# Last attention head with its softmax one step deeper, and the first expert's products in plain float32

## The reference

```python
logits = jnp.einsum('thd,tnhd->thn', q, k_sel).astype(jnp.float32) * ATT_HEAD_DIM ** -0.5
p = jax.nn.softmax(logits + bias, axis=-1)
o_att = jnp.einsum('thn,tnhd->thd', p, v_sel)
x = x + mix @ w_out                       # mix: retention heads and attention heads side by side
# for the 128 rows that an expert takes at a time:
hid = jax.nn.silu(xb @ w_gate[e]) * (xb @ w_up[e])
out = hid @ w_down[e]
```

## Time and profile before

| | |
|---|---|
| median of three runs | 1246.58 us (1245.07 to 1246.71) |
| the profiled execution's own time | 1249.32 us |
| its span in the trace | 1247.5 us |
| PE busy | 1137.8 us, 91% |
| DVE, ACT, POOL busy | 855.7, 692.5, 233.2 us |
| mean granted clock of PE | 0.958 of full |

### The profile page before, as it was taken

How to read it: one execution, slowest core, us unless ns; L and a number is a source line. 1 busy time by engine, 2 the same in 40 slices (tenths; PEclk the granted TensorE clock), 3 DMA queues, 4 the chain that set the end, 5 groups by cost and what they waited for, 6 DMA issues and landing times.

```text
span 1247.5 us, 18108 instructions
## 1 busy us (share of the span) xinstructions
PE 1137.8 (91%) x6481; PEld 938.6 (75%) x6481; DVE 855.7 (69%) x1763; ACT 692.5 (56%) x1191; POOL 233.2 (19%) x275
## 2 busy tenths in 40 slices
PE   5997899999999999999999789997699999999955
PEld 5984477888777987888887468886578888888832
DVE  6439878788888767333343532446899999999935
ACT  6347577787878142443433431113378888888822
POOL 1320024343333100000000000000233333343112
PEclk8999899999999899999999899997799999999978
DMA  8252030404030242444224534003699999999756
GB/s 283 41 118 28 29 98 1 110 1 110 1 87 1 58 131 60 111 119 109 78 70 133 170 105 179 34 35 135 224 403 397 397 386 395 394 391 391 285 206 279
DMA packets 129536, 205.35 MB, mean 165 GB/s; under 512 B 17396, under 2 KB 102804, under 8 KB 117156
## 3 DMA queue, kind: packets, MB, share of 16 engines
q1 hardware_dynamic: 114852, 177.61, 41.0%
q0 software_dynamic: 12864, 21.02, 5.4%
q10 hardware_dynamic: 1728, 5.51, 1.1%
HBM read 182.02 MB, written 34.37 MB: 173 GB/s over the span
## 4 chain that ended last, share of the span: by engine, by line
PE 76%; DVE 11%; ACT 4%; DMA 4%; issue 3%; SPq 1%; POOL 0%; DVEq 0%; POOLq 0%; ACTq 0%
PE psum L2239 5%; PE psum L2241 5%; PE psum L2512 5%; PE psum L2514 4%; PE psum L2240 4%; PE psum L2513 4%; DVE place L1481 3%; PE psum L2387 3%; PE psum L2389 3%; PE psum L2211 3%; PE psum L2388 3%; PE psum L2212 2%; PE psum L2213 2%; PE psum L2531 2%; PE psum L2533 2%
## 5 line engine op out<-in xcount | busy, mean ns | idle before, releaser
L1902 DVE TENSOR_TENSOR place<-place,place 128x2048 fp32r<-128x2048 f32 x64 | 146.2, 2286 | 9.8 <-ACT place L1272 9.8
L1095 ACT ACTIVATE place<-place,place 128x768 uint8<-128x768 f32 (+3 forms) x128 | 125.5, 983 | 6.7 <-DVE place L1512 6.7
L2239 PE MATMUL psum<-place,place 128*128 128x512 f32 x288 | 121.9, 423 | 2.4 <-DVE place L1469 2.4
L1272 ACT CAST place<-place 128x2048 fp32r<-128x2048 f32 x64 | 122.3, 1915 | 0.0
L2241 PE MATMUL psum<-place,place 128*128 128x512 f32 x288 | 113.4, 394 | 0.0
L2240 PE MATMUL psum<-place,place 128*128 128x512 f32 x288 | 112.6, 391 | 0.0
L2512 PE MATMUL psum<-place,place 128*128 128x512 f32 x256 | 106.7, 417 | 0.0
L2514 PE MATMUL psum<-place,place 128*128 128x512 f32 x256 | 101.4, 396 | 0.0
L2513 PE MATMUL psum<-place,place 128*128 128x512 f32 x256 | 101.0, 394 | 0.0
L2211 PE MATMUL psum<-place,place 128*128 128x256 f32 x288 | 87.1, 303 | 3.5 <-ACT place L1117 3.5
L905 POOL TENSOR_TENSOR place<-place,place 128x1 f32<-128x1 f32 x9 | 5.1, 565 | 428.1 <-DVE place L1862 428.1
(11 more groups left out here) (329 smaller groups left out, 3107.3 us busy)
## 6 DMA issues: line engine op xcount, KB each, us to landing
place<-in_w_gate SPq DMA_DIRECT2D x32, 1024.0 KB, 7.6
place<-in_w_up SPq DMA_DIRECT2D x32, 1024.0 KB, 9.9
place<-in_w_down SPq DMA_DIRECT2D x32, 1024.0 KB, 10.7
place<-in_w_in SPq DMA_DIRECT2D x28, 512.0 KB, 6.4
place<-expert_out SPq DMA_DIRECT2D x9, 1024.0 KB, 13.9
place<-in_cache_attn_k SPq DMA_DIRECT2D x32, 256.0 KB, 3.1
place<-in_cache_attn_v SPq DMA_DIRECT2D x32, 256.0 KB, 3.4
place<-in_x_prompt SPq DMA_DIRECT2D x3, 1536.0 KB, 6.9
```

Of the source, the lines that this page charges most:

```text
L1095: last = nc.scalar.activation(reached[j], score[j], ACT.Sign, bias=pivot.bitcast(F32)[:, j:j + 1], scale=-1.0, accum_out=minus[:, j - BY_A ...
L1272: nc.scalar.copy(w_gu_hi[e % 2][:, :, ks, :], w_gu[e % 3][:, :, ks, :]).then_inc(w_hi_done, 1)
L1902: nc.vector.tensor_tensor(w_gu_lo[e % 3][:, :, ks, :], w_gu[e % 3][:, :, ks, :], w_gu_hi[e % 2][:, :, ks, :].bitcast(F32), ALU.subtract).t ...
L2239: nc.tensor.matmul(bank(4 + b), hT_hi[:, k, rows], hi, start=k == 0, stop=False)
```

## The change

**Last head.** With `lag(h)` = 1 for the last head alone, PE turns the probabilities two steps after the logits and multiplies by the values three steps after. DVE scales step i-1 (`scaled`) behind the maximum of step i. A third buffer `prob_third` is used in turn with the two, and the turned rows go to PSUM banks 4 and 5 in turn (`turned_bank`). ACT copies a block's first four turned tiles ahead of the exponents and the rest behind them. The loop is one step longer. `high_mix(0)` and `low_mix(0)` move from step 7 to step 5, ahead of the output weights; the chunks are spread over steps 5 to 10; and chunk 7 alone stands behind the last block's values on PE, where 6 and 7 stood. `w_out` comes in two loads of 2 MB: one ahead of the first four cached values, one ahead of the last four, and `g_ffn` behind them all.

**First expert.** Its rows are copied, not split (ACT half of them, DVE the other half, from the two PSUM banks), and so are its hidden rows. Its weights are not split. PE takes 8 plain float32 products for 24, and 4 for 12, with the next expert's rows turned between the fourth and the fifth. DVE computes the gates ahead of the split of expert 1's weights, and `rows_lo(1)` stands behind `over_slots`.

```diff
@@ last head: PE
+                late = lag(h)
+                for i in range(T + 2 + late):
...
-                    if h + 1 == AH and i in (8, 9):
-                        first_out(OUT_FILL[i])
-                    if 1 <= i <= T:
-                        turn_probs(i - 1, 0)
+                    x = i - late
+                    if 1 <= x <= T:
+                        turn_probs(x - 1, 0)
...
+                    if x >= 2 and x - 2 != SAMPLE:
+                        values(x - 2)
...
+                    if h + 1 == AH and i in OUT_FILL:
+                        filled = first_out(OUT_FILL[i])
@@ tables
-        OUT_SPLIT = {5: (0, 1), 6: (2, 3), 7: (4,), 8: (5,), 9: (6, 7)}
-        OUT_FILL = {8: (0, 1, 2), 9: (3, 4, 5), 10: (6, 7)}
+        OUT_SPLIT = {5: (0, 1), 6: (2,), 7: (3, 4), 8: (5,), 9: (6,), 10: (7,)}
+        OUT_FILL = {8: (0, 1, 2), 9: (3, 4), 10: (5, 6), 11: (7,)}
@@ last head: SP
-                    sp.dma_start(w_out, i_["w_out"][0].rearrange("(c p) n -> p c n", p=P)).then_inc(w_out_in, 16)
-                    sp.dma_start(g_ffn, ...).then_inc(w_out_in, 16)
                 for i in range(NB, 2 * NB):
+                    if h + 1 == AH and i in (NB, LATE_VALUES):
+                        x = int(i == LATE_VALUES)
+                        sp.dma_start(w_out[:, 4 * x:4 * x + 4], ...).then_inc(w_out_in[x], 16)
                     load_cached(h, i)
+                if h + 1 == AH:
+                    sp.dma_start(g_ffn, ...).then_inc(w_out_in[1], 16)
@@ last head: DVE
+                    if late and 1 <= i <= T:
+                        scaled(i - 1)
...
+                    if h + 1 == AH and i == 5:
+                        low_mix(0)
                     if h + 1 == AH and i in OUT_SPLIT:
...
-                    if h + 1 == AH and i == 7:
-                        low_mix(0)
@@ first expert: DVE
-            gate_up_lo(0, 0)
-            gate_up_lo(0, 1)
             L(v, gates_of(1, *PARTS[1]))
             gates_of(2, *PARTS[2]).then_inc(frames_done, 1)
             gate_up_lo(1, 0)
+            gate_up_lo(1, 1)
...
-            rows_lo(0)
-            gate_up_lo(1, 1)
-            rows_lo(1)
+            raw_rows()
...
             over_slots()
+            rows_lo(1)
@@ first expert: PE
+            def raw_gate_up():
+                pe.wait_ge(xT_hi_done, 1)
+                pe.wait_ge(gu_in[0], 32)
+                for k in range(KD):
+                    if k == KD // 2:
+                        gathered(1)
+                    last = nc.tensor.matmul(bank(0), xT_over[:, k, :], w_gu[0][:, :, k, :], start=k == 0, stop=k == KD - 1)
+                last.then_inc(gu_ps, 1)
```

More of the change, by code:

```diff
@@ L1181, in turned_probs @@
                     w = min(4, key_tiles(ORDER[i]) - 4 * m)
-                    nc.scalar.copy(probT[i % 2][:, 4 * m:4 * m + w, :], bank(5, 0, w * P)).then_inc(tp_read, 1)
-                for i in range(T + 2):
+                    nc.scalar.copy(probT[i % 2][:, 4 * m:4 * m + w, :], turned_bank(h, i, m)[:, 0:w * P]).then_inc(tp_read, 1)
+                late = lag(h)
+                for i in range(T + 2 + late):
                     if i < 4:
                         cached_columns(2 * i)
+                    if late and 2 <= i <= T + 1:
+                        turned_probs(i - 2, 0)
                     if i < T:
@@ L1198, in attention @@
                         cached_columns(2 * i + 1)
-                    if 1 <= i <= T:
+                    if not late and 1 <= i <= T:
                         for m in range(GROUPS[i - 1]):
                             turned_probs(i - 1, m)
+                    if late and 2 <= i <= T + 1 and GROUPS[i - 2] == 2:
+                        turned_probs(i - 2, 1)
                     if i < 4 and h + 1 == AH:
@@ L1696, in attention, with scaled @@
                 bias_mask(ORDER[0])
-                for i in range(T + 3):
+                late = lag(h)
+                def scaled(i):
+                    w = P * key_tiles(ORDER[i])
+                    v.wait_ge(ex_done, T * h + i + 1)
+                    nc.vector.reciprocal(inv_sum[i % 2], row_sum[i % 2]).then_inc(rs_done, 1)
+                    v.wait_ge(rs_done, T * h + i + 1)
+                    nc.vector.tensor_scalar(prob_of(h, i)[:, 0:w], prob_of(h, i)[:, 0:w], inv_sum[i % 2], None, ALU.mult).then_inc(pn_done, 1)
+                for i in range(T + 3 + late):
                     if i < T:
@@ L2502, in hidden, with raw_down @@
                 turn_hidden(hid[e % 2]).then_inc(hid_ps, 1)
+            def raw_gate_up():
[6 more added lines that the diff above has]
+                last.then_inc(gu_ps, 1)
+            def raw_down():
+                pe.wait_ge(hidT_done, 1)
+                pe.wait_ge(dn_in[0], 16)
+                for half_n in range(2):
+                    for k in range(2):
+                        last = nc.tensor.matmul(bank(6 + half_n), hidT_over[:, k, :], w_dn[0][:, k, 512 * half_n:512 * half_n + 512],
+                                                start=k == 0, stop=k == 1)
+                last.then_inc(dn_ps, 1)
             def gate_up(e):
@@ L2536, in _ @@
             gathered(0)
-            for e in range(NE):
+            raw_gate_up()
+            for e in range(1, NE):
                 if e + 1 < NE:
@@ L2542, in _ @@
                     over_frames()
-                if e >= 1:
+                    raw_down()
+                else:
                     down(e - 1)
```

104 lines of the change are left out of this document (58 added, 46 removed).

## The result

The changed kernel takes 1237.05 us (median of 10 runs, 1232.59 to 1242.54), the kernel before, run beside it, 1247.26 (10 runs, 1243.39 to 1248.66): a ratio of 0.9918, 95% interval 0.9905 to 0.9932, so 10.2 us less (8.5 to 11.8). The forecast was 1237.7. The profiled execution took 1236.26 us, its span is 1234.4 and PE's mean granted clock 0.969, for 1249.32, 1247.5 and 0.958 before.

A forecast was written before the change was run, and what follows sets the result against it. PE was taken to bound the long stages, so gains had to come from its waits and half clock. Last head 6.0 plus first experts 2.9 gave 8.9 us off the median 1246.58: 1237.7, range 1233.5 to 1243.5.

The forecast's parts named there:

- The queue on DVE: Last head: DVE does `low_mix(0)`, two chunks and the maximum of step 6 ahead of the scale of step 5.
- the place and length of the wait: Last head: PE waits some 4 us for the scale of step 5, until 701.7.
- the 8.7 us from evacuation to the first turn with x: Behind the last head: fixed latency from last evacuation to PE's resuming with the sum, left unchanged, 8.7 us.
- 23.8 us at full clock: Last head: PE's own work behind the wait up to the last evacuation, 6.9 plus 16.9 us.
- the 3.0 us for half clock: Last head: PE's clock at half for some six us behind the 4 us wait, costing 3.0 us.
- the forecast's bound of 9.0: Last head: evacuation 9.0 us earlier if no time at half clock, against 6.0 forecast.
- Nothing between or behind is changed: Outside both changed stretches: the projection's tiles follow the first sum, the experts follow PE, with no further gain or loss.
- `down(1)` 2.9 us earlier: First experts: the second expert's down products start at 910.7 instead of 913.67, a gain of 2.9 us.
- Descriptors unchanged: First experts, rival: first gather's descriptors stay at 2.40 us, gain there 1.6 us, time 1239.0; chance 0.22.
- Half clock through the rest of the head: Last head, rival: half clock from 701.7 to 718 costs 8.2 us, not 3.0; time 1242.8; chance 0.11.
- Late values late: Last head, rival: the last four cached values land at 707.5, costing 3.0 us; time 1240.7; chance 0.06.
- Plain float32 keeps the clock down: Rival: plain float32 holds half clock; in experts only, 1248.6 us (chance 0.05); in head too, 1253.7 (0.04).

The follow-up runs named there:

- e7: Changed kernel plus four plain float32 products on PE in its wait for the scale of step 5 in the last head; 0.9910 of the kernel before.
- e6: Second run of the kernel before with only the change's first expert part, last head as before; 0.9990 of the kernel before.
- e2: Kernel before with only the change's first expert part, last head as before; 1.0011 of the kernel before.
- e1: Kernel before with only the change's last head part, experts as before; 0.9922 of the kernel before.
- e8: Changed kernel with DVE's gates behind the split of expert 1's weights instead of ahead of it; 0.9938 of the kernel before.
- e10: Changed kernel with both 2 MB loads of w_out ahead of all cached values of the last head; 0.9923 of the kernel before.
- e4: Changed kernel plus three plain float32 products on PE while it waits for the first gathered rows; 1234.13 us, 0.9902 of the kernel before.
- e11: Changed kernel with the last stage's identity products with x1 moved ahead of the waits for expert rows, some repeated; 0.9926 of the kernel before.
- e3: Changed kernel with earlier DVE scales and one chunk fewer at step 5 in the last head, w_out's second half behind late values; 0.9913 of the kernel before.
- e12: Changed kernel with early scales, w_out's second half behind late values, products ahead of first rows, and last-stage products ahead of waits; 0.9943 of the kernel before.

## Why the prediction was right, and where it wasn't

The forecast of 8.9 us came out at 10.2, inside its range, but not by its own terms: that it came so near is in part luck, as the sum below shows.

**The last head: mechanism right, a term mis-sized.** The queue on DVE, the place and length of the wait (3.73 us; forecast 4), no wait for cached values, the 8.7 us from evacuation to the first turn with x (8.64) all came as walked through. From the turn behind the wait to the last evacuation the walk had 23.8 us at full clock; e7, at full clock, has 23.95. The term that failed is the 3.0 us for half clock. The clock was at half for three us, not six, and e7 shows that it costs 0.6. So the head gained 8.5 (51.29 to 51.31 in all seven profiles of it), near the forecast's bound of 9.0, and not 6.0. One profile of before couldn't show that other engines' queues cover PE's clock there; a second could: e6's head takes 59.64 us with the clock up at 702 to 710, for 59.77 to 60.14 with it down.

**"Nothing between or behind is changed" was wrong.** The wait for x is as long as before (3.38 us for 3.42), but PE's clock didn't fall behind it: the turn takes 1.16 us, for 1.97 in e2, and the tiles 112.5 to 112.8 us for 114.0 to 114.1. That is 1.4 us more gain.

**The first expert: right up to the last scatter, then lost.** The forecast had `down(1)` 2.9 us earlier, and it came 2.6 earlier against the first gather; descriptors at 1.14, first plain product 2.73 us behind the rows (2.8), expert 1's turn without a wait. The sum failed where it took a gain in the experts for a gain in time. By e2 and e6 the part is worth nothing, with 1.1 us either way, because in the profiles the last stage is some 2 us longer with it. The prediction named no such rival: it looked at what is late next in the experts, not at the stage behind them. The mechanism of those 2 us is only half shown (the longer wait, and in three profiles the clock); the later landing itself stays open.

**The sum.** 8.5 of the head and 1.4 of the tiles make 9.9, and e1 measures 9.7; the experts add 2.8 and the last stage takes about 2.2 back. That makes 10.5 for a measured 10.2. Two errors of some 2.5 and 1.4 us one way and 2.2 or more the other cancelled in part, by luck.

**The rivals.** Descriptors unchanged: no (1.14; e8 brings 2.40 back by the order alone). Half clock through the rest of the head: no (1.88 us for block 7's logits). Late values late: no, and e10 shows slack even with all of `w_out` ahead of them. Plain float32 keeps the clock down: no (e4, e7). Two sums on record are off in the last digit, which changes nothing: half clock through the rest of the head leaves 9.0 - 8.2 = 0.8 us of gain and not 0.9, and the lower end of the range is 1246.58 - 13.3 = 1233.3 and not 1233.5.

## What to carry to other kernels

A wait on PE costs its own length and whatever half clock follows, but the second part counts only where no other engine's queue covers it; a second profile in which the clock happens not to fall tells that at once. A gain in one stage is a gain in time only when the last stage has been looked at too: time each part of a change alone, since the profile showed 2.8 us that the time didn't. Products put in to keep the clock up must end ahead of what PE waits for: 3.4 us in a wait of 3.7 made the head 0.6 us shorter; in e11 they ended 4.4 us behind the first rows and stood at 5.2 us for a later wait of 2.3, and the last stage grew by 2.6.

## What the hardware showed unexpectedly

**The clock behind the wait for x.** In all four profiles with the head as before PE's clock falls behind this wait, in all seven with the changed head it doesn't, and in e3, e7 and e12, whose heads differ from it only in the middle, it falls again. The wait is 3.05 to 3.57 us everywhere, and in the 12 us ahead of it PE is busy for 10.45 or 10.46 us in all ten, those where the clock falls and those where it doesn't. The turn behind the wait, e4's:

```profile
730.62 1.16 PE L2476 MATMUL psum<-place,place 128*128 128x128 f32 x8 [3.14 <-DVE place L1912]
```

and e7's:

```profile
732.52 1.97 PE L2479 MATMUL psum<-place,place 128*128 128x128 f32 x8 [3.57 <-DVE place L1912]
```

What decides it isn't known, and it is worth 1.3 to 2.4 us each time (tiles of 114.0 to 115.1 us, for a mean of 112.7 where it stays up).

**POOL's descriptors beside DVE's split.** The first two gathers take 1.14 and 1.03 us where DVE runs its short operations when they start, and 2.40 and 1.79 where the 4.5 us split of weights runs when they start, in all nine and all five profiles of either order. In the steady experts, where DVE splits nearly all the time, a gather takes longer again (all 32 together 2.24 us in the mean); there it hides behind PE.
